# Nine ring slots of weight halves in place of seven, seven of them for the dense part in place of five, and a DMA scratch of 512 bytes

## The chip, the cores and the metric

The kernel runs on one core of one Trainium2 chip. The metric is the device time of one execution in microseconds (us); it was taken in three runs. The core has TensorE (PE, matrix products), VectorE (DVE), ScalarE (ACT), GpSimd (POOL) and SyncE (SP), which here issues nearly all transfers. SBUF is the memory next to the engines, PSUM takes TensorE's results, HBM holds inputs, weights and output. A row of the profile names a line of the kernel file, as L419.

## The reference

Two decoder layers over 256 tokens of width 1024, all in float32. Each has a mixer (differential attention, dilated window attention and gated linear attention side by side), a cross-attention into 256 memory tokens, and a feed-forward part: a dense SwiGLU of width 2816 in layer 0, the best 2 of 8 expert SwiGLUs of width 3584 in layer 1. In short:

```python
for l in range(DEPTH):
    mix = hybrid_mixer(x, positions, w_in[l], ..., w_out[l])
    x = layer_norm(DEEPNORM_ALPHA * x + mix, ln_mix_g[l], ln_mix_b[l])
    xa = memory_cross_attention(x, mem, xa_wq[l], xa_wkv[l], xa_wo[l])
    x = layer_norm(DEEPNORM_ALPHA * x + xa, ln_xa_g[l], ln_xa_b[l])
    if l % 2 == 0:
        f = (silu(x @ w1) * (x @ w3)) @ w2        # ffd_w13, ffd_w2
    else:
        f = moe_swiglu(x, moe_router[0], moe_w13[0], moe_w2[0])
    x = layer_norm(DEEPNORM_ALPHA * x + f, ln_ffn_g[l], ln_ffn_b[l])
```

## The kernel before

The 256 tokens are two tiles of 128 (t = 0 and 1). Weights come in panels of 512 columns, and a panel in two **halves** of 1 MB: 128 partitions x 2048 elements, which is 8 KB per partition. The dense part (all of layer 0, and of layer 1 the mixer and the cross-attention) reads 99 halves, numbered 0 to 98 in `DENSE_HALVES`. Halves 24 to 27 are xa_wq of layer 0, 32 to 55 the up-projections of the dense layer (52 to 55 are only 256 columns wide), 56 to 66 its down-projection, 67 to 78 w_in of layer 1, and 95 to 98 xa_wo of layer 1. The expert part then reads, for each expert, 42 halves numbered q = 0 to 41.

All of them go through one buffer, `ring`, of `RAW_SLOTS` = 7 slots of 8 KB per partition. The dense part uses slots 0 to `DENSE_SLOTS` - 1 = 4. Slot 5 (`DENSE_SLOTS`) is meanwhile the first of four split buffers, `high`, and slot 6 (`RAW_SLOTS` - 1) is scratch room named `spare` (masks of the gated attention, the narrow weights of the forget gate). The expert part uses all 7 slots for its halves. `ring_r` is the same memory as `ring`, seen with the type float32r.

Most products are done in three passes on a split weight: w = w_hi + w_lo, both float32r. ACT casts a half to its high part (L532 in the dense part, into one of the four buffers `high`, whose names in rows are ring_r, late_r, late_r and qk_r; L553 in the expert part, into w_hi). DVE subtracts (L854, in place in the ring; L868, into w_lo). The key, value, w_out and xa_wo weights aren't split; TensorE reads them from the ring as they are. x is cast and subtracted likewise (L520 and L845) after TensorE has transposed it (L1384).

There is no scheduler: each engine runs its own list of instructions in program order, and semaphores order them against each other. What matters here:

- SP issues the halves in their order. `dense` waits, before half `at`, until half `at - DENSE_SLOTS` is used up (`wait_used`, L418). TensorE reports this by `dense_used`, `acc_ready`, `kv_psum` or `w2_ready`, whichever belongs to that half.
- At the end of the dense part SP issues the first six expert halves; those in slots 0 to 4 wait for the last dense half of their slot. Half 6 comes after `load_ln(5)`, which waits for the fifth layer norm (x2 of layer 1); slot 6 is scratch before. From half 7 on each waits for `lo_ready`: DVE has done the half 7 before.
- ACT casts a half once it has landed, and once the half that had its split buffer four split halves before is used up.
- In layer 1, DVE's list has the first expert subtraction, `low(0, 0)`, between the layer norm of tile 0 and the residual sums (L832) and layer norm (L816 to L823) of tile 1 after the cross-attention. ACT's list has three expert casts there, ahead of copying the transposes of x. Then come the router (L1772), the choice of experts, the gather (L1800), and the experts' products (L1819 to L1821).

The order in DVE's list there:

```python
                layer_norm(3 * l + 1, x, 0)
                if l == 0:
                    split_low(1)
                else:
                    low(0, 0)
                residual(l, o_p, 0, 1)
                if l == 0:
                    split_low(1)
                residual(l, o_p, 1, 1)
```

Of the kernel before, what the change touches and what calls it, by code (L numbers as in the profile page):

```python
# [22 lines left out]
F32R = mybir.dt.float32r  # L23
# [4 lines left out]
P = 128  # L28
# [3 lines left out]
KC = D // P  # L32
# [9 lines left out]
CH, CK, CV, CR = 4, 48, 96, 16  # L42
# [9 lines left out]
ROPE = 8  # L52

RAW_SLOTS = 7
DENSE_SLOTS = 5
SPLIT_SLOTS = 3
HALF = KC * N // 2

# [9 lines left out]
DENSE_HALVES = [(l, n, g) for l in range(DEPTH) for n in range(L1 if l == 0 else MIX_PANELS)  # L68
                for g in range(1 if n == L1 - 1 else 2)]
# [50 lines left out]
def bass_decoder(nc, a, out):  # L120
    ctx = ExitStack()
    with ctx:
        def sb(name, shape, dt=F32):
            return ctx.enter_context(nc.sbuf_tensor(name, shape, dt))

        def sem(name):
            return ctx.enter_context(nc.semaphore(name))
# [2 lines left out]


        with ExitStack() as scope:
            ring_r = scope.enter_context(nc.sbuf_tensor("ring_r", [P, RAW_SLOTS, HALF], F32R))
        ring = sb("ring", [P, RAW_SLOTS, HALF])
        ringf = ring[:, :, :].rearrange("p s n -> p (s n)")
        x = sb("x", [P, T, D])
        ln_gb = sb("ln_gb", [P, 2, D])
# [46 lines left out]
        with ExitStack() as scope:  # L184
            def twin(name, shape):
# [30 lines left out]
        o_xa = h[:, :, D:2 * D]  # L216
        cpad = sb("cpad", [P, T, 3 * CH, 64])
        qk = sb("qk", [P, 2, 2, 2 * S])
        spare = ring[:, RAW_SLOTS - 1, :]
        st = spare[:, 0:8 * P].rearrange("p (h b s) -> p h b s", h=2, b=4)  # L220
        stx = spare[:, 8 * P:12 * P].rearrange("p (h b s) -> p h b s", h=2, b=2)

        high = (ring_r[:, DENSE_SLOTS, :], late_r[:, 8192:10240], late_r[:, 12288:14336],
                qk_r[:, :, :, :].rearrange("p m n s -> p (m n s)"))
# [13 lines left out]
        angr = sb("angr", [P, 2, T, ROPE])  # L238
        trig = sb("trig", [P, 2, T, ROPE])
        rt = s4[:, 0, :, 0:T * 24 * 4].rearrange("p n (t k) -> p n t k", t=T)  # L240
        wr_hi, wr_lo = (ring_r[:, RAW_SLOTS - 1, m * KC * CR:(m + 1) * KC * CR].rearrange("p (c r) -> p c r", c=KC)
                        for m in range(2))
        rankT = spare[0:CR, 14 * P:16 * P]
        zz = dec[:, 0:3, 0:T * CH * CK]
# [13 lines left out]
        ln_in = sem("ln_in")  # L258
        dense_in = [sem(f"dense_in{s}") for s in range(DENSE_SLOTS)]
        dense_used = sem("dense_used")  # L260
# [64 lines left out]
        def acc_use(l, n):  # L325
            return l * L1_ACC + (n if n < IN_P else n - KV_P)
# [17 lines left out]
        def dense_src(l, n, g):  # L344

            src = w_panel(l, n)
            c = 2 if n >= L1 - W2_P else 4
            return src[:, c * g:c * (g + 1), :]

        def dense_view(buffer, l, n, g):  # L350
            _, c, w = dense_src(l, n, g).shape
            return buffer[:, 0:c * w].rearrange("p (c n) -> p c n", c=c)

        def raw_half(l, n, g):
            return dense_view(ring[:, HALF_AT[l, n, g] % DENSE_SLOTS, :], l, n, g)

# [3 lines left out]
        def low_half(l, n, g):  # L360
            return dense_view(ring_r[:, HALF_AT[l, n, g] % DENSE_SLOTS, :], l, n, g)

        def half_view(buffer, q, slots):

            return buffer[:, q % slots, :].rearrange("p (c n) -> p c n", c=4 if q < 4 * MOE_PAIRS else 2)
# [13 lines left out]
        def wait_used(engine, index):  # L379


            l, n, g = DENSE_HALVES[index]
            if n == L1 - 1:
                engine.wait_ge(w2_ready, T)
            elif g == 0 or n >= L1 - W2_P:
                own = sum(1 for m, k, c in DENSE_HALVES[:index + 1] if (c == 0 or k >= L1 - W2_P) and k != L1 - 1)
                engine.wait_ge(dense_used, own)
            elif IN_P <= n < IN_P + KV_P:
                engine.wait_ge(kv_psum, 2 * KV_P * l + 2 * (n - IN_P) + 2)
            else:  # L390
                u = acc_use(l, n)
                engine.wait_ge(acc_ready[2 * (u % 2) + 1], u // 2 + 1)
# [8 lines left out]
        @block.sync  # L401
        def _(sp):
            sp.dma_start(x[:, :, :], a["x"][0].rearrange("(t p) d -> p t d", p=P)).then_inc(x_in, 16)
            sp.dma_start(square[:, :, :], a["square"]).then_inc(x_in, 16)

            def load_ln(k):
                l, s = divmod(k, 3)
                g, b = (("ln_mix_g", "ln_mix_b"), ("ln_xa_g", "ln_xa_b"), ("ln_ffn_g", "ln_ffn_b"))[s]
                if k:
                    sp.wait_ge(ln_done, T * k)  # L410
                for n, w in enumerate((g, b)):
                    sp.dma_start(ln_gb[:, n, :], a[w][l:l + 1, :].to_broadcast([P, D])).then_inc(ln_in, 16)

            def dense(l, n):
                for g in range(1 if n == L1 - 1 else 2):
                    at = HALF_AT[l, n, g]
                    if at >= DENSE_SLOTS:
                        wait_used(sp, at - DENSE_SLOTS)  # L418
                    sp.dma_start(raw_half(l, n, g), dense_src(l, n, g)).then_inc(dense_in[at % DENSE_SLOTS], 16)  # L419

            for l in range(DEPTH):
                for n in range(L1 if l == 0 else MIX_PANELS):
                    dense(l, n)
                    if l == 0 and n == 1:
                        sp.dma_start(mem_tok, a["mem"][0].rearrange("(t p) d -> p t d", p=P)).then_inc(mem_in, 16)
                    if n == IN_P + KV_P + OUT_P - 1:
                        load_ln(3 * l)
                    if n == MIX_PANELS - 1:
                        load_ln(3 * l + 1)
                    if n == L1 - 1:  # L430
                        load_ln(3 * l + 2)

            def item_half(q, i, e):

                if q < 4 * MOE_PAIRS:
                    c0 = (q // 2 % 2) * F_MOE + q // 4 * N
                    r = 4 * (q % 2)
                    src = a["moe_w13"][0, e].rearrange("(c p) n -> p c n", p=P)[:, r:r + 4, c0:c0 + N]
                else:
                    r = 2 * (q - 4 * MOE_PAIRS)  # L440
                    src = a["moe_w2"][0, e].rearrange("(c p) n -> p c n", p=P)[:, r:r + 2, :]
                sp.dma_start(half_view(ring, q, RAW_SLOTS), src).then_inc(raw_in[q % RAW_SLOTS], 16)

            def item_halves(i, e, first=0):
                for q in range(first, ITEM_HALVES):
                    sp.wait_ge(lo_ready, ITEM_HALVES * i + (q - RAW_SLOTS + 1))
                    item_half(q, i, e)


            for q in range(RAW_SLOTS - 1):  # L450
                if q < DENSE_SLOTS:
                    last = max(i for i in range(len(DENSE_HALVES)) if i % DENSE_SLOTS == q)
                    wait_used(sp, last)
                item_half(q, 0, 0)
            load_ln(5)
            item_half(RAW_SLOTS - 1, 0, 0)
            item_halves(0, 0, RAW_SLOTS)
            with sp.Fori(1, NE) as i:
                item_halves(i, i)
            sp.wait_ge(table_ready, 1)  # L460
            n_items = sp.value_load(table_i[0:1, 0:1], min_val=NE, max_val=NE + EXTRA)
            with sp.If(n_items > NE):
                with sp.Fori(NE, n_items) as i:
                    e = sp.value_load(table_i[0:1, bass.ds(i - (NE - 1), 1)], min_val=0, max_val=NE - 1)
                    item_halves(i, e)
            sp.wait_ge(ln_done, T * 6)
            sp.dma_start(out[0].rearrange("(t p) d -> p t d", p=P), acc).then_inc(out_done, 16)
            sp.wait_ge(out_done, 16)
# [1445 lines left out]
```

## Time and profile before

| what | value |
|---|---|
| median of three runs | 1912.48 us |
| lowest and highest run | 1912.01 and 1916.35 us |
| span of the profiled execution (first to last instruction) | 1910.2 us |
| busy: PE, DVE, ACT, POOL | 94%, 68%, 51%, 1% |
| mean granted TensorE clock | 0.968 |
| HBM over the span | 244 GB/s |
| transfers of dense halves, issue to landing | about 5.0 us each |

The page gives the span of the profiled execution; its time as a run is not listed apart, and no run is below 1912.01 us. Busy shares are means over stages with different limits: in the first 860 us or so, the dense part, transfers take some 10 to 60% of the DMA engines' time in all slices but the first, and after it 90% and more in most. What a slot of the ring is worth must be read at the single places where an engine waits for a transfer. A row of the chain of waits gives a start, a duration and what ran; where the next row starts at once, the step was released by the one before it. In a timeline the bracket at the end of a row is the idle time of the engine before it, and what ended it.

### The profile page before, as it was taken

The numbers are of one execution on the slowest core, as the hardware profiler recorded it, in microseconds if no ns is written. First come the engines' busy times: TensorE is split into PE (matmuls) and PEld (weight loads), VectorE is DVE, ScalarE is ACT, GpSimd is POOL, SyncE is SP. The second block draws the span as 40 slices with busy tenths as digits, with TensorE's granted clock in tenths as the row PEclk, the third lists the DMA queues.
The fourth block names the chain that finished last, engine by engine and source line by source line (L and its number), as shares of the span: only waits on it lengthen the run. The fifth ranks groups of instructions, "written<-read, shape, count | busy, mean of one in ns | idle before, by whom it ended". The sixth has DMA issues, their size and how long they took to land.

```text
span 1910.2 us, 21467 instructions
## 1 busy us (share of the span) xinstructions
PE 1791.2 (94%) x7962; PEld 1385.8 (73%) x7962; DVE 1298.7 (68%) x1209; ACT 975.6 (51%) x853; POOL 13.8 (1%) x22
## 2 busy tenths in 40 slices
PE   7998889999899989979999999999999999999996
PEld 6846575788776475647887878878878778788785
DVE  4465434445463555258988888889889788898896
ACT  4333122444333312216766667667667676676673
POOL 0000000000000000000000000000000000000000
PEclk9998899999999969979999999999999999999998
DMA  8523232545534312267999989999999999999991
GB/s 283 177 88 111 67 132 88 180 173 186 211 132 153 112 67 88 89 242 255 363 348 322 370 321 344 338 327 371 339 324 371 332 331 335 326 370 341 322 370 63
DMA packets 206471, 466.19 MB, mean 244 GB/s; under 512 B 11952, under 2 KB 14416, under 8 KB 206416
## 3 DMA queue, kind: packets, MB, share of 16 engines
q1 hardware_dynamic: 200880, 463.76, 67.7%
q10 hardware_dynamic: 5536, 1.68, 0.4%
q8 instruction: 36, 0.59, 0.1%
q14 instruction: 19, 0.16, 0.0%
HBM read 464.36 MB, written 1.05 MB: 244 GB/s over the span
## 4 chain that ended last, share of the span: by engine, by line
PE 85%; DVE 6%; ACT 4%; issue 4%; DMA 1%; POOL 0%; DVEq 0%; SPq 0%; ACTq 0%
PE ps L1423 21%; PE ps L1819 15%; PE ps L1821 15%; PE ps L1820 15%; PE ps L1450 6%; PE ps L1741 3%; ACT w_hi L553 3%; PE ps L1809 1%; PE ps L1800 1%; PE ps L1614 1%; DVE w_lo L868 1%; PE ps L1831 1%; PE ps L1667 1%; PE ps L1649 1%; PE ps L1384 1%
## 5 line engine op out<-in xcount | busy, mean ns | idle before, releaser
L868 DVE TENSOR_TENSOR w_lo<-ring,w_hi 128x2048 fp32r<-128x2048 f32 x336 | 768.6, 2289 | 163.9 <-ACT w_hi L553 163.4
L553 ACT CAST w_hi<-ring 128x2048 fp32r<-128x2048 f32 x336 | 641.7, 1910 | 329.9 <-PE ps L1821 316.8
L1819 PE MATMUL ps<-w_hi,xe_hi 128*128 128x512 f32 x896 | 364.5, 407 | 2.7 <-DVE xe_lo L1271 1.4
L1821 PE MATMUL ps<-w_hi,xe_lo 128*128 128x512 f32 x896 | 349.7, 390 | 0.0
L1820 PE MATMUL ps<-w_lo,xe_hi 128*128 128x512 f32 x896 | 348.9, 389 | 0.0
L1819 PEld LDWEIGHTS ps<-w_hi,xe_hi 128*128 128x128 f32 x896 | 168.3, 188 | 43.4 <-issue 8.3
L1820 PEld LDWEIGHTS ps<-w_lo,xe_hi 128*128 128x128 f32 x896 | 168.4, 188 | 40.0 <-issue 6.7
L1821 PEld LDWEIGHTS ps<-w_hi,xe_lo 128*128 128x128 f32 x896 | 168.1, 188 | 36.1
L1819 PE MATMUL ps<-w_hi,he_hi 128*128 128x512 f32 x448 | 177.5, 396 | 0.0
L1821 PE MATMUL ps<-w_hi,he_lo 128*128 128x512 f32 x448 | 174.8, 390 | 0.0
L1820 PE MATMUL ps<-w_lo,he_hi 128*128 128x512 f32 x448 | 174.4, 389 | 0.0
L1423 PE MATMUL ps<-ring_r,xT_r 128*128 128x512 f32 (+1 forms) x560 | 149.4, 398 | 11.7 <-DVE late_r L845 6.8
L1423 PEld LDWEIGHTS ps<-ring_r,xT_r 128*128 128x128 f32 x560 | 105.3, 193 | 35.9 <-DVE late_r L845 7.6
L1423 PE MATMUL ps<-ring,xT 128*128 128x512 f32 x256 | 116.1, 611 | 9.3 <-ACT xT L510 6.3
L1450 PE MATMUL ps<-ring,memT 128*128 128x512 f32 x256 | 116.4, 598 | 0.1
L1423 PEld LDWEIGHTS ps<-ring,xT 128*128 128x128 f32 x256 | 49.8, 197 | 69.3 <-issue 62.5
L1821 PEld LDWEIGHTS ps<-w_hi,he_lo 128*128 128x128 f32 x448 | 84.1, 188 | 18.0
L1820 PEld LDWEIGHTS ps<-w_lo,he_hi 128*128 128x128 f32 x448 | 84.3, 188 | 16.6
L1819 PEld LDWEIGHTS ps<-w_hi,he_hi 128*128 128x128 f32 x448 | 84.2, 188 | 16.4
L532 ACT CAST late_r<-ring 128x2048 fp32r<-128x2048 f32 (+1 forms) x34 | 63.0, 1858 | 63.1 <-DMA ring<-in_xa_wq_dram 20.4
L854 DVE TENSOR_TENSOR ring_r<-ring,late_r 128x2048 fp32r<-128x2048 f32 (+1 forms) x34 | 75.5, 2227 | 27.1 <-ACT late_r L532 26.2
L1450 PEld LDWEIGHTS ps<-ring,memT 128*128 128x128 f32 x256 | 46.2, 190 | 50.9 <-issue 49.5
(258 smaller groups left out, 1834.3 us busy)
## 6 DMA issues: line engine op xcount, KB each, us to landing
ring<-in_moe_w_dram SPq DMA_DIRECT2D x336, 1024.0 KB, 5.0
ring<-in_ffd_w_dram SPq DMA_DIRECT2D x31, 1024.0 KB, 5.0
ring<-in_w_in_dram SPq DMA_DIRECT2D x24, 1024.0 KB, 5.1
ring<-in_xa_wkv_dram SPq DMA_DIRECT2D x16, 1024.0 KB, 4.9
ring<-in_w_out_dram SPq DMA_DIRECT2D x8, 1024.0 KB, 5.0
ring<-in_xa_wq_dram SPq DMA_DIRECT2D x8, 1024.0 KB, 5.0
ring<-in_xa_wo_dram SPq DMA_DIRECT2D x8, 1024.0 KB, 5.1
ring<-in_ffd_w_dram SPq DMA_DIRECT2D x4, 512.0 KB, 3.6
```

The costliest lines, as they stand in the source:

```text
L532: act.copy(high_half(*name), raw_half(*name)).then_inc(dense_hi, 1)
L553: act.copy(w_hi[:, q % SPLIT_SLOTS, :], ring[:, q % RAW_SLOTS, :]).then_inc(hi_ready, 1)
L854: dve.tensor_tensor(low_half(*name), raw_half(*name), high_half(*name).bitcast(F32), ALU.subtract).then_inc(dense_lo, 1)
L868: dve.tensor_tensor(w_lo[:, q % SPLIT_SLOTS, :], ring[:, q % RAW_SLOTS, :], w_hi[:, q % SPLIT_SLOTS, :].bitcast(F32), ALU.subtract).then_i ...
L1384: ins = pe.transpose(ps[:, 4 + b, c * P:(c + 1) * P], src[:, t, k * P:(k + 1) * P], ident)
L1423: ins = pe.matmul(ps[:, b, 0:w], lhs[:, 4 * g + c, t * P:(t + 1) * P], rhs[:, c, :], start=(g == 0 and m == 0 and c == 0), stop=(g == 1 an ...
L1450: ins = pe.matmul(ps[:, piece_bank(i), :], memT[:, k, t * P:(t + 1) * P], raw_half(l, IN_P + n, g)[:, c, :], start=(k == 0), stop=(k == KC ...
L1614: ins = pe.matmul(ps[:, 4 + 2 * hp + s % 2, at:at + P], k[:, t * P:(t + 1) * P], q[:, tq * P:(tq + 1) * P], start=True, stop=True)
L1741: ins = pe.matmul(ps[:, t + 2 * col, :], (h_hi, h_lo)[p][:, k, t * P:(t + 1) * P], weights[q][:, c, col * N:(col + 1) * N], start=(k == 0 ...
L1819: pe.matmul(ps[:, bank, :], x_hi, hi[:, c, cols], start=first, stop=False)
L1820: pe.matmul(ps[:, bank, :], x_hi, lo[:, c, cols], start=False, stop=False)
L1821: return pe.matmul(ps[:, bank, :], x_lo, hi[:, c, cols], start=False, stop=last)
```

## The change

- `DENSE_SLOTS` is 7, and a new `RING_SLOTS` = `DENSE_SLOTS` + 2 = 9 is the size of `ring` and `ring_r`: 16 KB per partition more. The dense part goes round over slots 0 to 6. The split buffer `high[0]` is slot 7, and `spare` slot 8.
- `RAW_SLOTS` stays 7: the expert part uses slots 0 to 6.
- The first seven expert halves now each wait for the last dense half of their slot, and all seven come before `load_ln(5)`.
- The DMA scratch (`dynamic_dma_scratch_size`) is set to 512 bytes, where the argument was left at its default.

```diff
--- before.py
+++ after.py
@@ -52,7 +52,8 @@
 ROPE = 8
 
 RAW_SLOTS = 7
-DENSE_SLOTS = 5
+DENSE_SLOTS = 7
+RING_SLOTS = DENSE_SLOTS + 2
 SPLIT_SLOTS = 3
 HALF = KC * N // 2
 
@@ -130,8 +131,8 @@
 
 
         with ExitStack() as scope:
-            ring_r = scope.enter_context(nc.sbuf_tensor("ring_r", [P, RAW_SLOTS, HALF], F32R))
-        ring = sb("ring", [P, RAW_SLOTS, HALF])
+            ring_r = scope.enter_context(nc.sbuf_tensor("ring_r", [P, RING_SLOTS, HALF], F32R))
+        ring = sb("ring", [P, RING_SLOTS, HALF])
         ringf = ring[:, :, :].rearrange("p s n -> p (s n)")
         x = sb("x", [P, T, D])
         ln_gb = sb("ln_gb", [P, 2, D])
@@ -216,7 +217,7 @@
         o_xa = h[:, :, D:2 * D]
         cpad = sb("cpad", [P, T, 3 * CH, 64])
         qk = sb("qk", [P, 2, 2, 2 * S])
-        spare = ring[:, RAW_SLOTS - 1, :]
+        spare = ring[:, RING_SLOTS - 1, :]
         st = spare[:, 0:8 * P].rearrange("p (h b s) -> p h b s", h=2, b=4)
         stx = spare[:, 8 * P:12 * P].rearrange("p (h b s) -> p h b s", h=2, b=2)
 
@@ -238,7 +239,7 @@
         angr = sb("angr", [P, 2, T, ROPE])
         trig = sb("trig", [P, 2, T, ROPE])
         rt = s4[:, 0, :, 0:T * 24 * 4].rearrange("p n (t k) -> p n t k", t=T)
-        wr_hi, wr_lo = (ring_r[:, RAW_SLOTS - 1, m * KC * CR:(m + 1) * KC * CR].rearrange("p (c r) -> p c r", c=KC)
+        wr_hi, wr_lo = (ring_r[:, RING_SLOTS - 1, m * KC * CR:(m + 1) * KC * CR].rearrange("p (c r) -> p c r", c=KC)
                         for m in range(2))
         rankT = spare[0:CR, 14 * P:16 * P]
         zz = dec[:, 0:3, 0:T * CH * CK]
@@ -447,13 +448,11 @@
                     item_half(q, i, e)
 
 
-            for q in range(RAW_SLOTS - 1):
-                if q < DENSE_SLOTS:
-                    last = max(i for i in range(len(DENSE_HALVES)) if i % DENSE_SLOTS == q)
-                    wait_used(sp, last)
+            for q in range(RAW_SLOTS):
+                last = max(i for i in range(len(DENSE_HALVES)) if i % DENSE_SLOTS == q)
+                wait_used(sp, last)
                 item_half(q, 0, 0)
             load_ln(5)
-            item_half(RAW_SLOTS - 1, 0, 0)
             item_halves(0, 0, RAW_SLOTS)
             with sp.Fori(1, NE) as i:
                 item_halves(i, i)
@@ -1899,7 +1898,7 @@
     import concourse.bacc as bacc
     from concourse.bass_utils import run_bass_kernel_spmd as run
 
-    nc = bacc.Bacc("TRN2", target_bir_lowering=False, num_devices=1)
+    nc = bacc.Bacc("TRN2", target_bir_lowering=False, num_devices=1, dynamic_dma_scratch_size=512)
     given = {name: np.ascontiguousarray(inputs[name]) for name in _INS}
     given.update(shape_constants())
     arrays, args = {}, {}
```

ACT, DVE, TensorE and GpSimd keep their instructions and their order; what changes for them is which slot and which of now seven `dense_in` semaphores a half has. SP's list changes at every wait of the dense part, in the same way: it waits for the half 7 before, not 5 before. Two places of it follow.

SP's queue from the last narrow up-projection halves to the first w_in halves of layer 1, before:

```order
L419 DMA ring<-in_ffd_w13_dram 128x4x256 [waits acc_ready1]
L419 DMA ring<-in_ffd_w13_dram 128x4x256 [waits dense_used]
L419 DMA ring<-in_ffd_w2_dram 128x2x1024 [waits acc_ready3]
L419 DMA ring<-in_ffd_w2_dram 128x2x1024 [waits dense_used]
L419 DMA ring<-in_ffd_w2_dram 128x2x1024 [waits acc_ready1]
L419 DMA ring<-in_ffd_w2_dram 128x2x1024 [waits dense_used]
L419 DMA ring<-in_ffd_w2_dram 128x2x1024 [waits acc_ready3]
L419 DMA ring<-in_ffd_w2_dram 128x2x1024 [waits dense_used] x6
L412 DMA ln_gb<-in_ln_ffn_g_dram 128x1024 [waits ln_done]
L412 DMA ln_gb<-in_ln_ffn_b_dram 128x1024
L419 DMA ring<-in_w_in_dram 128x4x512 [waits dense_used] x4
L419 DMA ring<-in_w_in_dram 128x4x512 [waits w2_ready]
```

The same place of the changed kernel (line numbers are one higher):

```order
L420 DMA ring<-in_ffd_w2_dram 128x2x1024 [waits acc_ready1]
L420 DMA ring<-in_ffd_w2_dram 128x2x1024 [waits dense_used]
L420 DMA ring<-in_ffd_w2_dram 128x2x1024 [waits acc_ready3]
L420 DMA ring<-in_ffd_w2_dram 128x2x1024 [waits dense_used]
L420 DMA ring<-in_ffd_w2_dram 128x2x1024 [waits acc_ready1]
L420 DMA ring<-in_ffd_w2_dram 128x2x1024 [waits dense_used]
L420 DMA ring<-in_ffd_w2_dram 128x2x1024 [waits acc_ready3]
L420 DMA ring<-in_ffd_w2_dram 128x2x1024 [waits dense_used] x4
L413 DMA ln_gb<-in_ln_ffn_g_dram 128x1024 [waits ln_done]
L413 DMA ln_gb<-in_ln_ffn_b_dram 128x1024
L420 DMA ring<-in_w_in_dram 128x4x512 [waits dense_used] x6
L420 DMA ring<-in_w_in_dram 128x4x512 [waits w2_ready]
```

Each half now carries the wait that the half two places ahead of it carried before: of the w_in halves six instead of four wait for `dense_used`, that is for halves inside the down-projection, ahead of the one that waits for its end (`w2_ready`).

SP's queue at the end of the cross-attention of layer 1, where the expert halves begin (in_moe_w13), before:

```order
L412 DMA ln_gb<-in_ln_xa_g_dram 128x1024 [waits ln_done]
L412 DMA ln_gb<-in_ln_xa_b_dram 128x1024
L442 DMA ring<-in_moe_w13_dram 128x4x512 [waits dense_used]
L442 DMA ring<-in_moe_w13_dram 128x4x512 [waits acc_ready1]
L442 DMA ring<-in_moe_w13_dram 128x4x512 [waits dense_used]
L442 DMA ring<-in_moe_w13_dram 128x4x512 [waits acc_ready3] x2
L442 DMA ring<-in_moe_w13_dram 128x4x512
L412 DMA ln_gb<-in_ln_ffn_g_dram 128x1024 [waits ln_done]
L412 DMA ln_gb<-in_ln_ffn_b_dram 128x1024
L442 DMA ring<-in_moe_w13_dram 128x4x512
L442 DMA ring<-in_moe_w13_dram 128x4x512 [waits lo_ready] x21
```

The same place of the changed kernel:

```order
L413 DMA ln_gb<-in_ln_xa_g_dram 128x1024 [waits ln_done]
L413 DMA ln_gb<-in_ln_xa_b_dram 128x1024
L443 DMA ring<-in_moe_w13_dram 128x4x512 [waits acc_ready3]
L443 DMA ring<-in_moe_w13_dram 128x4x512 [waits acc_ready1]
L443 DMA ring<-in_moe_w13_dram 128x4x512 [waits dense_used]
L443 DMA ring<-in_moe_w13_dram 128x4x512 [waits acc_ready3]
L443 DMA ring<-in_moe_w13_dram 128x4x512 [waits dense_used]
L443 DMA ring<-in_moe_w13_dram 128x4x512 [waits acc_ready1]
L443 DMA ring<-in_moe_w13_dram 128x4x512 [waits dense_used]
L413 DMA ln_gb<-in_ln_ffn_g_dram 128x1024 [waits ln_done]
L413 DMA ln_gb<-in_ln_ffn_b_dram 128x1024
L443 DMA ring<-in_moe_w13_dram 128x4x512 [waits lo_ready] x21
```

The first expert half waited for `dense_used` of half 95, the first half of the last but one panel. Now it waits for `acc_ready3`, which TensorE gives at its last product of the dense part (half 98). The other six waits are for halves 92 to 97, and the seventh half stands ahead of the layer norm weights.

## Rows read from the trace of the kernel before

**Rows 1.** The page, part 4: the chain by engine

```profile
PE 85%; DVE 6%; ACT 4%; issue 4%; DMA 1%; POOL 0%; DVEq 0%; SPq 0%; ACTq 0%
```

**Rows 2.** The chain, 430 to 545: start us, us, what

```profile
445.44 4.92 DMA ring<-in_ffd_w_dram
...
456.04 4.31 PE ps L1741 x12
...
516.48 5.41 DMA ring<-in_w_in_dram
...
521.91 1.90 ACT late_r L532
...
524.41 0.70 DVE late_r L845
...
525.80 13.54 PE ps L1423 x48
```

**Rows 3.** The chain, 821 to 841

```profile
821.43 4.89 DMA ring<-in_moe_w_dram
...
826.40 1.91 ACT w_hi L553
...
828.34 2.29 DVE w_lo L868
...
837.73 1.96 PE ps L1384 x8
```

**Rows 4.** Waits, 0 to 850 and 860 to 1910: us, times, longest us

```profile
PE ps L1423 <- DVE late_r L845: 17.5, 8, 5.7
...
ACT w_hi L553 <- PE ps L1821: 316.8, 331, 5.2
```

**Rows 5.** SP's timeline (start, us, what); landings of its first, then of the next two

```profile
831.73 1.47 SPq L442 DMA_DIRECT2D ring<-in_moe_w_dram  x3
...
DMA to landing us min/median/max: 5.1/5.1/5.1
...
DMA to landing us min/median/max: 7.3/8.4/9.5
```

**Rows 6.** Windows: us, PE PEld DVE ACT POOL busy (x), PEclk, DMA share, GB/s

```profile
525.00:530.00 5.00, 4.20 (x10) 3.37 (x11) 5.00 (x4) 0.00 (x0) 0.00 (x0) 0.50 0.01 3
...
840.00:845.00 5.00, 4.45 (x21) 4.48 (x22) 4.80 (x3) 0.00 (x0) 0.00 (x0) 0.50 1.03 388
```

**Rows 7.** Timeline of DVE from 450: start us, us, what, idle before

```profile
452.32 2.29 DVE L854 TENSOR_TENSOR ring_r<-ring,late_r 128x2048 fp32r<-128x2048 f32 x1 [0.68 <-ACT late_r L532]
```

**Rows 8.** Timeline of SP's queue, from 446.5 and from 496

```profile
446.86 0.37 SPq L419 DMA_DIRECT2D ring<-in_ffd_w_dram  x1
...
496.97 0.38 SPq L419 DMA_DIRECT2D ring<-in_w_in_dram  x1
```

**Rows 9.** Timeline of DVE from 519

```profile
519.26 0.69 DVE L1216 SCALAR_TENSOR_TENSOR x<-x,ps 128x512 f32<-128x512 f32 x1 [2.29 <-PE ps L1741]
...
521.43 0.69 DVE L1217 BATCH_NORM_STATS2 stats<-x 128x6 f32<-128x512 f32 x1
```

**Rows 10.** Timelines of ACT from 231 and of DVE from 237

```profile
231.88 1.90 ACT L532 CAST late_r<-ring 128x2048 fp32r<-128x2048 f32 x1 [20.38 <-DMA ring<-in_xa_wq_dram]
...
237.18 0.69 DVE L832 SCALAR_TENSOR_TENSOR x<-x,ps 128x512 f32<-128x512 f32 x1 [1.00 <-PE ps L1423]
```

**Rows 11.** The chain at 43, and ACT's timeline from 27

```profile
43.18 44.57 PE ps L1423 x192
...
27.14 5.04 ACTq L570 DMA_DIRECT2D ring<-in_w_in_dram  x2
...
35.09 1.91 ACT L532 CAST ring_r<-ring 128x2048 fp32r<-128x2048 f32 x1 [0.17 <-ACT h L498]
```

**Rows 12.** The page, part 3: the two queues that carry the kernel's data

```profile
q1 hardware_dynamic: 200880, 463.76, 67.7%
...
q10 hardware_dynamic: 5536, 1.68, 0.4%
```

## The prediction

> **What bounds the kernel now.** I read the chain that ended last first, then the waits, then the transfers' issue and landing times at the places where a transfer stands on that chain. The chain is 85% TensorE and only 1% DMA [rows 1]. A deeper ring of weight slots can give back only what stands there as DMA, or what ACT and DVE do late because of it. The reader is to see three such places: 445.44 (a half of the dense layer's down-projection), 516.48 (first weights of the second layer) and 821.43 (first expert weights) [rows 2, 3]. Behind the last one comes the expert part, more than half of the span; there ACT waits 316.8 us in 331 pieces for TensorE to free a split buffer [rows 4], so ring and transfers are ahead of TensorE and the part shifts as a whole with its start. It keeps 7 slots in both kernels.
>
> **The hand-over to the experts, the largest term.** What changes is which dense half had the slot before. The 99 dense halves are numbered 0 to 98, and a half goes to the slot of its number modulo the dense slots. With 5, expert half 0 takes slot 0 after half 95, half 1 follows 96, half 2 follows 97, half 3 follows 98. With 7, slot 0 held half 98, the very last one; expert halves 1 to 6 follow 92 to 97, but stand behind half 0 in SP's queue. So all seven wait until TensorE has finished the last dense product.
> When is that? Half 95 is used up at 821.43, where expert half 0 is issued [rows 3]; half 98 at 831.73, where SP issues half 3, which waits for it today, and two more [rows 5]. The first expert transfer moves by 831.73 - 821.43 = 10.30 us.
> What hangs on it: the transfer (4.89), ACT's cast to w_hi (1.91 from 826.40), DVE's subtraction to w_lo (2.29 from 828.34), and behind that in DVE's queue both residual sums of token tile 1 and its layer norm, then TensorE's transposes at 837.73 [rows 3]. Each step follows the one before at once, and TensorE's last product, which the second sum needs, is over by then. No slack absorbs the delay: +10.30. Router, top-2 choice, gather and all experts come after.
> Does the landing change with seven transfers queued? Three are issued today within 1.47 us from 831.73: the first lands after 5.1 us, at 836.8, the third after 9.5 us, by 842.2, so they are some 2.7 us apart [rows 5]. The first does not wait for those behind it. Half 0 then lands at 836.8, half 2 at 842.2, and ACT is through its three casts at 844.1, before the transposes of x, at 837.73 + 10.30 = 848.0, need it. I take 0; the upper bound is 9.5 - 5.1 = 4.4 us, as if the first landed like the third.
> The Trainium skill (DMA: Bandwidth & Descriptors, Bandwidth) gives 6.15 us for a 1 MB transfer from HBM. By that figure half 0 would land 1.05 us later than by the row, and the hand-over would cost an estimated 11.4 us in place of 10.3; the row has 5.1 us, and it decides.
> SP goes on to the norm weights and half 7 once the layer norm is done, 10.3 us later too; TensorE's expert start moves as far, so the lead of the ring stays.
>
> **The longer TensorE pause there.** The idle stretch before 837.73 grows by 10.3 us. In 840 to 845, behind today's pause, the granted clock is already 0.50, that is 1.2 GHz [rows 6]; the router and the gather run behind a fallen clock in both kernels. I take 0, with 1.7 us either way for a fall or rise that comes earlier or later.
> The Trainium skill (TensorE: Matmul & The Clock Gate, What's actually happening) has the throttled clock as the default, released by activity, which speaks against a change that makes TensorE idle longer. By that rule the loss would exceed the shift only if work behind today's pause ran at the full clock; the row shows that it does not.
>
> **What the dense part wins.** Each half is issued once the half 7 before it, not 5 before it, is used up: two halves earlier.
> At 445.44 half 57 is issued, and lands 4.92 later [rows 2]. With 7 slots it goes two halves sooner; its split buffer is free when half 53 is used up, at 446.86 [rows 8], so ACT can cast right behind its previous cast. Today DVE idles 0.68 us for that cast before its subtraction at 452.32 [rows 7]; then come the gating products that free the last PSUM bank, and TensorE starts at 456.04 [rows 2]. With the transfer gone DVE is the bound: -0.68.
> At 516.48 half 70 is issued, once half 65 is used; it lands after 5.41, ACT casts for 1.90 from 521.91 and then casts x; DVE subtracts x at 524.41, and TensorE starts at 525.80 [rows 2]. With 7 slots half 69 goes at 496.97, where 67 goes today [rows 8], and half 70 when half 63 is used. From half 65 used (516.48) to half 66 used (519.26 [rows 9]) is 2.78 us, so half 63 is used at 510.9 and half 70 lands by 516.4. Next late is the split buffer: there are four, so the cast of half 70 waits for half 66, at 519.26, when DVE also gets its residual sums [rows 9]. ACT ends that cast at 521.2 and the first x cast some 0.6 later; DVE is busy with sums and statistics until 521.43 + 0.69 = 522.12 [rows 9]. So DVE's x subtraction starts at 522.15 in place of 524.41: -2.26.
> TensorE's granted clock is 0.50 in 525 to 530 [rows 6]. The 48 products from 525.80 take 13.54 us, and 192 of that kind take 44.57 at the start, so 48 would take 11.1 [rows 2, 11]. Started 2.3 us sooner, TensorE may meet more or less of the slow stretch: 2.4 us at most are to be won, and I set 1.7 as the loss. I take 0.
>
> **Where it wins nothing.** ACT waits 20.38 us for a half of xa_wq before 231.88. But DVE's residual sum at 237.18 waits for TensorE, not for ACT, whose cast is long done [rows 10]. The second layer has the same code.
> At the start two more ring transfers go out at once. They use the engines for 2 x 2.7 = 5.4 us while ACT issues its constants (the last two end at 27.14 + 5.04). If that held ACT up by all of it, its cast of 35.09 would end at 42.4, DVE's subtraction at 44.7, and the products of 43.18 would start 1.5 us late [rows 11]. Value 0, upper bound 1.5, nothing below.
> The scratch: all kernel data goes by q1 and q10, both hardware_dynamic (463.76 and 1.68 MB) [rows 12], issued by SP and ACT; GpSimd issues none. I take 0 for 512 bytes; a loss would show as slower landings everywhere.
>
> **Sum.** +10.30 - 0.68 - 2.26 = +7.36 us. The profiled span is 1910.2, the median of the runs 1912.48; the 2.3 us between them are taken to lie around the span and stay. 1912.48 + 7.36 = 1919.8 us.
>
> **Rivals.** A, the forecast: 1917.4 (2.4 us of clock won) to 1923.2 (1.7 us lost at both places). Chance 0.63, of which 0.10 comes out within 0.3% (5.7 us, about what a measurement here can tell from no change).
> B, the dense part wins nothing, because something that I count as ready, a split buffer or DVE's queue, is late in place of the transfer: +10.30, 1922.8. For it: four split buffers against seven slots. Against: DVE's rows at 519 to 522 [rows 9]. Chance 0.14.
> C, a dear start (+1.5) or shared landing (+4.4) on top of the sum: 1921.3 to 1924.2. Against the second: the landings at 831.73 [rows 5]. Chance 0.08.
> D, not slower: TensorE waits 17.5 us in 8 places for DVE's x subtraction at the layer norms [rows 4]. If there the transfers hold ACT and DVE up, the deeper ring shortens all eight. From 7.4 us on, less than half of it, that pays for the hand-over; at 10 us the sum is -2.6, 1909.8. For it: ACT's wait of 20.38 us right before one of the places. Against: DVE waits for TensorE at 237.18 [rows 10]. Chance 0.15, 0.06 of it faster, 0.09 within.
> Faster 0.06, same 0.10 + 0.09 = 0.19, slower 0.75. Range 1915.0 to 1924.5: down into D and the clock, up over B and C.
>
> **What would show it.** Right: SP's first expert transfer starts where TensorE's last dense product ends, near 828.8 (831.73 - 2.94); its half lands 4.9 to 5.2 us after; ACT, DVE and TensorE follow in today's order. TensorE starts the down-projection near 455.4 and the second layer near 522.9. ACT's 20 us wait for xa_wq is gone and the layer norm behind it comes no sooner. The expert part takes as long as before. Wrong: the second layer's start stays put (B), the gaps at the layer norms shrink (D), or half 0 lands over 6 us after its issue (C).

## The result, and the profile after

| kernel | median us | runs | ratio to the kernel before, 95% interval |
|---|---|---|---|
| before, beside it | 1912.24 | 4 | |
| changed | 1922.47 | 4 | 1.0045 (1.0032 to 1.0057) |
| before, beside the repeat | 1913.93 | 21 | |
| changed, repeated | 1920.37 | 5 | 1.0037 (1.0024 to 1.0051) |

The change makes the kernel slower, by 8.6 us (6.1 to 10.9) in the first comparison and by 7.1 us (4.6 to 9.8) in the repeat, working the ratios out on the two medians of before. The forecast was 1919.8 us, 7.4 us slower. The ratios are those on record and aren't the quotients of the medians: the medians in this table differ by 10.2 and 6.4 us.

The hand-over to the experts, in the chain of the changed kernel (start us, us, what); it answers to [rows 3]:

```profile
818.76 13.98 PE ps L1422 x32
...
832.76 5.06 DMA ring<-in_moe_w_dram
...
837.90 1.91 ACT w_hi L552
...
839.84 2.29 DVE w_lo L867
...
849.23 1.95 PE ps L1383 x8
...
852.05 6.98 PE ps L1771 x32
```

The reader is to see that the chain now goes through all 32 instructions of the last dense products and only then to the transfer: it starts at 832.76, where TensorE ends. Before, it left TensorE after 8 of them, at 821.43. From the start of these products to the router it takes 852.05 - 818.76 = 33.29 us, and took 22.82 (817.73 to 840.55 in the chain of before): +10.47.

Seven transfers go out together now. SP's timeline of the changed kernel from 832, and the landings of the first two and of the second and third, which answer to [rows 5]:

```profile
832.76 6.86 SPq L443 DMA_DIRECT2D ring<-in_moe_w_dram  x6
...
DMA to landing us min/median/max: 5.1/6.2/7.4
...
DMA to landing us min/median/max: 7.4/8.4/9.5
```

The first still lands after 5.1 us, the second after 7.4, the third after 9.5. It does not wait for those behind it.

The dense layer and the start of the second layer, in the chain of the changed kernel; it answers to [rows 2]:

```profile
443.70 5.66 PE ps L1422 x48
...
449.94 1.92 ACT ring_r L531
...
454.09 2.28 DVE ring_r L853
...
457.80 4.58 PE ps L1740 x12
...
521.29 0.70 DVE x L1215
...
523.46 0.70 DVE stats L1216
...
524.19 0.70 DVE late_r L844
...
525.58 12.98 PE ps L1422 x48
```

No row with DMA stands in this stretch any more. At both places DVE works without a gap up to TensorE's start: the second subtraction (454.09) right behind the first, and x's subtraction (524.19) right behind the statistics.

The waits of the changed kernel, 0 to 850 and from 865 (us, times, longest us), answering to [rows 4]:

```profile
PE ps L1422 <- DVE late_r L844: 15.2, 8, 3.5
ACT w_hi L552 <- DMA ring<-in_moe_w_dram: 22.0, 3, 20.5
...
ACT w_hi L552 <- PE ps L1820: 316.9, 331, 5.1
```

TensorE's waits at the layer norms fell from 17.5 to 15.2 us, and the longest of them from 5.7 to 3.5: the 2.3 us are the second layer's start alone. ACT's one long wait for a transfer is now the hand-over. Its wait for TensorE in the expert part is what it was.

Two rows of ACT in the changed kernel, at xa_wq of layer 0 (it answers to [rows 10]) and at the start of the second layer:

```profile
240.09 1.07 ACT L519 CAST xT_r<-ps 128x512 fp32r<-128x512 f32 x2 [24.75 <-PE ps L1383]
...
523.15 1.07 ACT L519 CAST xT_r<-ps 128x512 fp32r<-128x512 f32 x2
```

In the first, ACT waits for TensorE's transposes of x, no longer for a transfer. In the second, two casts of x take 1.07 us together, so I estimate that the first is done near 523.7, while DVE takes x up at 524.19: ACT, and with it the split buffer that it had to wait for, is ahead of DVE there by about 0.5 us.

### The profile page after: what moved, and what is told of

It is laid out like the page before. It is cut to its first block, busy times and chain, and to the rows that moved or that the text cites. A ratio compares the mean times of both kernels' runs of the same rounds, so it can differ in the third digit from the quotient of the medians.

```text
span 1920.9 us, 21467 instructions
## 1 busy us (share of the span) xinstructions
PE 1796.0 (93%) x7962; PEld 1388.1 (72%) x7962; DVE 1297.9 (68%) x1209; ACT 974.7 (51%) x853; POOL 13.8 (1%) x22
## 4 chain that ended last, share of the span: by engine, by line
PE 85%; DVE 7%; ACT 4%; issue 3%; DMA 1%; POOL 0%; DVEq 0%; SPq 0%; ACTq 0%
PE ps L1422 22%; PE ps L1818 15%; PE ps L1820 14%; PE ps L1819 14%; PE ps L1449 6%; PE ps L1740 3%; ACT w_hi L552 3%; PE ps L1808 1%; PE ps L1613 1%; DVE w_lo L867 1%; PE ps L1799 1%; PE ps L1830 1%; PE ps L1666 1%; PE ps L1648 1%; PE ps L1383 1%
## 5 line engine op out<-in xcount | busy, mean ns | idle before, releaser
L552 ACT CAST w_hi<-ring 128x2048 fp32r<-128x2048 f32 x336 | 641.7, 1910 | 339.0 <-PE ps L1820 316.9
L1449 PE MATMUL ps<-ring,memT 128*128 128x512 f32 x256 | 120.3, 615 | 0.1
L853 DVE TENSOR_TENSOR ring_r<-ring,late_r 128x2048 fp32r<-128x2048 f32 (+1 forms) x34 | 75.3, 2225 | 18.5 <-ACT late_r L531 17.5
```

The source lines that it names most:

```text
L552: act.copy(w_hi[:, q % SPLIT_SLOTS, :], ring[:, q % RAW_SLOTS, :]).then_inc(hi_ready, 1)
L853: dve.tensor_tensor(low_half(*name), raw_half(*name), high_half(*name).bitcast(F32), ALU.subtract).then_inc(dense_lo, 1)
L1449: ins = pe.matmul(ps[:, piece_bank(i), :], memT[:, k, t * P:(t + 1) * P], raw_half(l, IN_P + n, g)[:, c, :], start=(k == 0), stop=(k == KC ...
```

## Where the time went, in stretches of all profiles

Every profile's chain has the same landmarks: (a) the 192 products that begin near 43 us, (b) the first products of the dense layer, (c) of its down-projection, (d) of the second layer, (e) the run of 240 products in it, (f) the last 32 product instructions of the dense part, (g) the router. Differences of their starts, in us; the names of the experiments are those of the next section:

| profile | slots | a to b | b to c | c to d | d to e | e to f | f to g |
|---|---|---|---|---|---|---|---|
| before | 5 | 280.0 | 132.83 | 69.76 | 16.27 | 275.66 | 22.82 |
| e9 (before again) | 5 | 282.5 | 132.83 | 70.02 | 16.22 | 275.65 | 22.97 |
| e2 (scratch) | 5 | 282.6 | 132.92 | 70.24 | 16.21 | 275.65 | 23.01 |
| e3 (late wait) | 5 | 282.6 | 132.99 | 69.94 | 16.34 | 275.74 | 33.31 |
| changed | 7 | 282.8 | 132.09 | 67.78 | 15.70 | 277.48 | 33.29 |
| e5 (changed again) | 7 | 279.6 | 133.63 | 67.79 | 15.70 | 276.92 | 33.42 |
| e1 (turned by 1) | 7 | 281.1 | 132.08 | 67.77 | 15.68 | 276.81 | 22.58 |
| e7 (turned by 6) | 7 | 281.1 | 132.04 | 67.79 | 15.70 | 276.81 | 29.84 |
| e4 (six slots) | 6 | 282.2 | 132.05 | 67.80 | 15.70 | 275.64 | 26.49 |
| e6 (six, turned) | 6 | 282.5 | 132.03 | 67.78 | 15.70 | 274.02 | 22.53 |
| e8 (five split buffers) | 6 | 280.3 | 132.22 | 66.34 | 16.54 | 277.56 | 22.54 |

The columns b to c, c to d, d to e and f to g follow the kernel to half a microsecond, save where a slow clock stretch falls otherwise (b to c in e5, c to d and d to e in e8, told below). The column a to b does not follow it: it differs by 3.2 us between the two profiles of the changed kernel, and by 2.5 between those of the kernel before. The column e to f differs by 0.6 and 0.0 us between the same pairs, and by 3.5 between e6 and e8, which have the same dense slots; both are taken up in the section on the prediction.

## The experiments

**e1: the change, with expert half q in ring slot (q + 1) mod 7.** Half 98's slot then goes to expert half 6.

```diff
-            return buffer[:, q % slots, :].rearrange(...)
+            at = (q + TURN_BY) % slots if slots == RAW_SLOTS else q % slots
+            return buffer[:, at, :].rearrange(...)
-                last = max(i for i in ... if i % DENSE_SLOTS == q)
+                last = max(i for i in ... if i % DENSE_SLOTS == (q + TURN_BY) % RAW_SLOTS)
```

(and the same index where ACT and DVE read the ring; `TURN_BY` = 1)

> The change with one difference: expert half q takes ring slot (q + 1) mod 7 in place of q mod 7, so that the slot of the last dense half (98) goes to expert half 6, and halves 0 to 5 follow dense halves 92 to 97. Theory (the hand-over costs the change 10.3 us because expert half 0 waits for half 98): the first expert transfer is issued well before TensorE's last dense product, ACT does not wait for it, and DVE's second residual sum follows that product at once, some 0.3 us sooner after it than in the kernel before. The rest is the dense part's win, 2.0 to 3.3 us. Time 3 us below the kernel before (1908 to 1910.5) and 11 to 13 us below the change. Rival (the loss comes from the deeper ring itself, by slower or shared transfers, or from clock stretches that the changed dense part brings about): no more than half of the 10 us is regained, the time stays above 1915.

Measured: 1910.16 us against 1914.49, ratio 0.9975 (0.9966 to 0.9984). That is 4.8 us faster than before, and 12 to 13 us below the change by the ratios. Its chain at the hand-over:

```profile
816.50 13.99 PE ps L1424 x32
...
830.60 0.70 DVE x L833
...
836.26 1.95 PE ps L1385 x8
...
839.08 6.98 PE ps L1773 x32
```

and ACT's timeline there, where the bracket at the end is the idle time before:

```profile
815.07 5.51 ACT L554 CAST w_hi<-ring 128x2048 fp32r<-128x2048 f32 x3
830.95 0.58 ACT L511 COPY xT<-ps 128x512 f32<-128x512 f32 x1 [10.37 <-PE ps L1385]
```

No transfer stands on the chain. ACT casts all three halves at once at 815, 1.4 us before the last dense products begin, and DVE's second residual sum follows TensorE's end by 0.1 us. The stretch f to g is 22.58 us, 10.7 below the change's and 0.2 to 0.4 below that of the three undelayed profiles with five slots. With the 3.6 us of b to e that makes 4.0 us by the stretches; the runs have 4.8 (3.1 to 6.5). This shows that the loss was the slot order, not the deeper ring.

**e2: the kernel before, with the scratch of 512 bytes alone.**

```diff
-    nc = bacc.Bacc("TRN2", target_bir_lowering=False, num_devices=1)
+    nc = bacc.Bacc("TRN2", target_bir_lowering=False, num_devices=1, dynamic_dma_scratch_size=512)
```

> The kernel before with the DMA scratch of 512 bytes alone, ring untouched. Theory: no difference, within 0.2% of the kernel before, transfers landing after 4.9 to 5.1 us as there. Rival (the scratch is part of the loss): 2 to 10 us slower, landings above 5.3 us.

Measured: 1917.19 us against 1914.49, ratio 1.0009 (1.0000 to 1.0019), that is 1.8 us (0 to 3.6): the interval touches no difference. The runs lie in two groups, four from 1912.06 to 1914.74 us and six from 1917.16 to 1917.99, and the profile is of a run of the first (1914.35). Its transfers, from part 6 of its page (the last number is the median from issue to landing), took 0.0 to 0.3 us longer than before:

```profile
ring<-in_moe_w_dram SPq DMA_DIRECT2D x336, 1024.0 KB, 5.2
ring<-in_ffd_w_dram SPq DMA_DIRECT2D x31, 1024.0 KB, 5.2
ring<-in_w_in_dram SPq DMA_DIRECT2D x24, 1024.0 KB, 5.4
```

That is above the 4.9 to 5.1 us expected, but e9, which has the old scratch, shows 5.1, 5.1 and 5.3 in these rows, and e3, also with the old scratch, 5.2, 5.2 and 5.3: the excess does not belong to the scratch. In its stretches b to g it stands within 0.25 us of e9, the kernel before again, each. A loss of 2 us or more that belongs to the scratch is not seen in any stretch of this profile. By the runs alone up to 3.6 us are not excluded; against as much stand e1, e6 and e8, which have the small scratch and are 4 to 5 us faster than the kernel before, no less than the 4 us that their shorter stretches give.

**e3: the kernel before, where expert half 0 waits for dense half 98 in place of 95.**

```diff
-                    wait_used(sp, last)
+                    wait_used(sp, last if q else len(DENSE_HALVES) - 1)
```

> The kernel before, five dense slots, seven in all, with one wait changed: expert half 0 waits for dense half 98 in place of 95. Theory: this wait alone is the cost of the hand-over, 10.3 to 10.7 us, with none of the dense part's win: 1922 to 1923.5. Rival (part of the step is due to seven transfers at once, or the dense part already lags): under 8 us.

Measured: 1923.27 us against 1914.49, ratio 1.0052 (1.0038 to 1.0066), so 10.0 us (7.3 to 12.6). The stretch f to g is 33.31 us, the same as the change's 33.29:

```profile
820.51 13.99 PE ps L1423 x32
...
834.52 5.07 DMA ring<-in_moe_w_dram
```

One wait, in a kernel with five slots and the old scratch, costs the whole hand-over. The columns from b to e stay at the five-slot values.

**e4: the change with six dense slots, eight in all.**

```diff
-DENSE_SLOTS = 7
+DENSE_SLOTS = 6
-                last = max(i for i in ... if i % DENSE_SLOTS == q)
-                wait_used(sp, last)
+                if q < DENSE_SLOTS:
+                    last = max(i for i in ... if i % DENSE_SLOTS == q)
+                    wait_used(sp, last)
```

(expert half 6, whose slot held a split buffer, has no wait of its own; it stands in SP's queue behind the waits of the others)

> The change with six dense slots, eight in all. Dense halves are then issued one later than in the change, one earlier than before; expert half 0 waits for half 96, half 1 for 97, half 2 for 98. Theory: hand-over 3.44 us late (half 96 used at 824.87 against 821.43), the same win in the dense part, since half 70 then lands at 519.1, just as its split buffer comes free: sum 0 to +1.5 us against the kernel before. Rival (depth itself costs, in proportion): half of the change's loss, +5 us.

Measured: 1914.09 us against 1914.49, ratio 1.0001 (0.9992 to 1.0010). Its chain at the hand-over:

```profile
815.41 7.12 PE ps L1423 x16
822.55 5.12 DMA ring<-in_moe_w_dram
...
841.90 6.98 PE ps L1772 x32
```

The chain leaves TensorE after 16 of the 32 instructions, once half 96 is used up: f to g is 26.49, 3.5 us above the 22.93 that is the mean of before, e9 and e2. The dense part's win is there in full, and the two cancel.

**e5: the changed kernel once more.** No edit.

> The changed kernel itself once more, beside more runs of the kernel before on the same chip. The first comparison gave +0.45% (0.32 to 0.57), more than the forecast sum of 7.4 us. Theory (the sum is right and the rest was chance, TensorE's slow clock stretches falling otherwise in single executions): +0.3 to +0.45%, 6 to 9 us, and in its profile the stretch from 43 us to the start of the dense layer does not always carry the 2.5 us that it carried in the first profile. Rival (the deeper ring itself slows the mixers, by about 2.5 us): +0.5% or more, and the first 325 us as long as in the first profile.

Measured: 1920.37 us, ratio 1.0037 (1.0024 to 1.0051); the stretch a to b took 279.6 us, 3.2 less than in the first profile of the same kernel. The windows of 105 to 125 us of the changed kernel's two profiles and of e9, one line each in that order (PE, PEld, DVE, ACT, POOL busy, then the granted clock):

```profile
105.00:125.00 20.00, 18.29 (x69) 9.28 (x68) 11.02 (x33) 5.86 (x20) 0.00 (x0) 0.91 0.32 106
```

```profile
105.00:125.00 20.00, 18.29 (x72) 9.37 (x71) 12.41 (x35) 5.92 (x21) 0.00 (x0) 1.00 0.29 106
```

```profile
105.00:125.00 20.00, 18.28 (x69) 9.33 (x68) 11.02 (x33) 5.71 (x20) 0.00 (x0) 0.91 0.32 106
```

In the first profile of the change and in e9, but not in e5 nor in the first profile of before (where the same window shows 1.00), the clock fell for a moment here, and TensorE got through 69 instructions in place of 72. The rival, a ring that slows the mixers, falls for this stretch. Between b and c it is the other way round: the 48 products at b take 12.95 us in e5, with the clock at 0.86 in 320 to 325, and 11.40 us in the first profile, with 1.00; that is the 1.5 us by which b to c is longer in e5.

**e6: six dense slots, and half q in slot (q + 3) mod 7.** The edit is shown against e1.

```diff
-DENSE_SLOTS = 7
-TURN_BY = 1
+DENSE_SLOTS = 6
+TURN_BY = 3
```

(slot 6, the first split buffer, waits for the last split half that lay in it)

> Six dense slots, eight in all, and expert half q in slot (q + 3) mod 7, so that half 98's slot goes to expert half 6. Theory: hand-over as in the turned version with seven dense slots, and the dense part's win is the same with six slots as with seven, since the four split buffers bound it: the same time as the turned version, 3 to 5 us below the kernel before (ratio 0.997 to 0.9985). Rival (each slot more gives its own share): half the win, ratio 0.9985 or above.

Measured: 1909.14 us against 1913.93, ratio 0.9979 (0.9970 to 0.9988). The dense columns are those of seven slots. With the turned order six slots do what seven do, with 8 KB per partition less.

**e7: seven dense slots, turned by six.** Expert half 0 follows half 97. The edit is shown against e1.

```diff
-TURN_BY = 1
+TURN_BY = 6
```

> Seven dense slots, expert half q in slot (q + 6) mod 7: expert half 0 follows dense half 97, which is used up 3.43 us before half 98, and half 1 follows half 98. Theory (the cost is the distance of the half that expert half 0 waits for, nothing else): hand-over 6.9 us later than in the kernel before in place of 10.3, less 3.3 us of win in the dense part: +3 to +4.5 us against the kernel before, 3.4 us below the change. Rival (what counts is that all seven are queued behind TensorE's end, or several land late together): as slow as the change, +8 us.

Measured: 1917.38 us against 1913.93, ratio 1.0020 (1.0011 to 1.0029), 3.8 us. Its chain:

```profile
816.35 10.55 PE ps L1424 x24
826.91 5.05 DMA ring<-in_moe_w_dram
...
846.19 6.98 PE ps L1773 x32
```

24 of the 32 instructions, then the transfer; f to g is 29.84. Against the mean of 22.93, waiting for half 96, 97 or 98 costs 3.56 (e4), 6.91 (e7) and 10.36 to 10.49 us (changed, e5), where the experiments' expectations had 3.44 and 6.9 and the prediction 10.30. All seven are queued one behind the other in e7 too; only the half waited for differs.

**e8: e6 with a fifth split buffer.**

```diff
-RING_SLOTS = DENSE_SLOTS + 2
-HIGH_SLOTS = 4
+RING_SLOTS = DENSE_SLOTS + 3
+HIGH_SLOTS = 5
-        high = (ring_r[:, DENSE_SLOTS, :], late_r[:, 8192:10240], ...
+        high = (ring_r[:, DENSE_SLOTS, :], ring_r[:, DENSE_SLOTS + 1, :], late_r[:, 8192:10240], ...
-                    by_tile = last + 1 - HIGH_SLOTS
+                    by_tile = last + 1 - 4
```

(the last edit keeps TensorE's order of the down-projection as it was)

> The six-slot turned version with a fifth split buffer (nine slots in all), so that the cast of the last half for the second layer waits for half 65 in place of 66 and is 2.8 us sooner. Theory (DVE's residual sums and statistics after the down-projection end as late as ACT's cast chain, and bound TensorE's start): no gain, TensorE starts the second layer 67.8 us after the down-projection as with four buffers, time as the six-slot turned version (ratio 0.997 to 0.999 to the kernel before). Rival (the split buffer is what is late next): another 1 to 2.5 us there.

Measured: 1910.00 us against 1914.30, ratio 0.9976 (0.9966 to 0.9986), as e6. In the profile c to d is 66.34, 1.4 less than the expected 67.8, but the buffer does not give it. Its chain at the start of the down-projection:

```profile
455.79 3.04 PE ps L1744 x12
...
459.26 58.55 PE ps L1744 x252
```

The first 12 products take 3.04 us, where the changed kernel's row of 457.80 has 4.58: no slow clock there this time (1.00 over 455 to 462, against 0.76). Behind d it is the other way round: 48 products take 13.82 us against 12.98, which makes d to e longer. From the 252 products on it is 522.13 - 459.26 = 62.87 us, against 525.58 - 462.81 = 62.77 in the changed kernel. DVE's timeline of e8 at that place:

```profile
520.01 0.69 DVE L1220 BATCH_NORM_STATS2 stats<-x 128x6 f32<-128x512 f32 x1
520.74 1.29 DVE L848 TENSOR_TENSOR late_r<-ps,xT_r 128x512 fp32r<-128x512 f32 x2
```

x's subtraction follows the statistics without a gap: DVE is the bound. With six slots ACT's casts there wait for their transfers again (3.33 and 1.54 us before the last two), so the run does not show what a fifth buffer does beside seven.

**e9: the kernel before once more, one profile.** No edit.

> The kernel before once more, one profile, to see how TensorE's slow clock stretches fall in another execution of the same program. Theory (they fall by chance): the stretch from 43 us to the dense layer's first product differs from the first profile's 280.0 us by 1 to 2.5 us, with slow stretches at other places, while the pieces between differ by less than 0.2 us. Rival (they are fixed by the program): the same places as in the first profile.

Measured: 1914.02 us, span 1912.2. The stretch a to b is 282.5 us against 280.0, and its slow clock at 105 to 125 us stands above. The four columns between b and f agree within 0.26 us between the two profiles, a little more than the 0.2 expected, and within 0.5 us over the four profiles with five slots.

## Why the prediction was right, step by step

- **Hand-over, +10.30.** Right. The profiles have +10.47 from the first profile of before, and 10.36 to 10.49 from the mean of three. e3 shows it by one wait alone, e1 by taking it away, e4 and e7 by its steps. The small excess is the landing: the changed kernel's transfer takes 5.06 us where before had 4.89 [rows 3]. The 11.4 us that the prediction works out beside it from the Trainium skill (DMA: Bandwidth & Descriptors, Bandwidth) is not a rival sum: the table of that section is for transfers issued from GpSimd, where SP issues these, and a slower landing would stand in the chain of both kernels and leave the shift as it is.
- **Landings with seven queued, 0.** Right: 5.1, 7.4 and 9.5 us, as of three [rows 5]. The 4.4 us of the upper bound did not come.
- **The longer pause of TensorE, taken as 0.** No loss came. The 0.8 us by which the next item is shorter are in the gather: its 32 products take 5.88 us in the first profile of the change against 6.72 before. The pause does not set this: e3, with the same late hand-over, has 6.60, as e9 without it has 6.59. It lies within the bound of 1.7.
- **Expert part, unchanged.** Right: from the router to DVE's last normalizing instruction 1063.0 us against 1063.8 before, and ACT's wait for TensorE 316.9 against 316.8 us. From the router to the end of the span it is 1068.8 to 1069.7 us in all eleven profiles.
- **Down-projection, -0.68.** 132.06 us (mean of changed, e1, e4, e6, e7) against 132.89 (before, e9, e2, e3) from b to c: -0.83. DVE's idle time of 0.68 [rows 7] is gone, as the chain after shows.
- **Second layer's start, -2.26.** 67.78 against 69.99: -2.21. The step that names what is late next was right too: DVE's sums and statistics, which end about 0.5 us after ACT's first cast of x, and so after all that the split buffer holds up (ACT's row of 523.15 above).
- **The clock behind it, taken as 0.** Mis-sized. From d to e it is 15.70 against 16.26 us, -0.56: started sooner, the 48 products take 12.98 in place of 13.54. It lies within the bounds of -2.4 and +1.7.
- **Nothing at xa_wq, at the start, or elsewhere.** ACT's 20 us wait is gone; instead it waits 24.75 us for TensorE's transposes of x before its next cast, at 240.09. The layer norm behind it comes no sooner: a to b takes 279.6 to 282.8 us with seven slots and 280.0 to 282.6 with five, and what differs there is TensorE's own time, as shown below. Nor does the start lose: a lies at 42.66 to 43.05 us with seven slots, at 42.39 to 43.18 with five. The stretch e to f needs a closer look: 277.5, 276.9, 276.8 and 276.8 us in four profiles with seven slots, 275.6 to 275.7 in five with five or six, but 274.0 and 277.6 in two others with six. Adding up the chain's pieces by engine settles where this is. In all eleven profiles DVE's pieces take 24.18 to 24.21 us there, ACT's 6.02 to 6.04 and the pieces named issue 7.29 to 7.33; only TensorE's differ, from 234.5 us (e6) to 238.0 (changed, e8), with 236.1 before. So nothing waits longer or less; the same products take longer or less. Two pairs of rows show it, each before and then changed, the second pair with e5:

```profile
661.83 5.35 PE ps L1450 x12
```

```profile
662.09 7.58 PE ps L1449 x12
```

```profile
751.63 12.94 PE ps L1423 x48
```

```profile
751.68 11.40 PE ps L1422 x48
```

The granted clock is 1.00 and 0.74 over 655 to 665 in the first pair, 0.89 and 1.00 over 750 to 765 in the second. The stretch a to b is of the same kind: DVE 26.28 to 26.32 us, ACT 6.01 to 6.05 and issue 7.82 to 7.86 in all eleven, TensorE 237.4 (e5) to 240.7 (changed). What stays open is whether the deeper ring has a part in where the clock falls: e5, e1 and e7 are alike from e to f, but the first profile of the change is like e8, with six slots.

- **Sum.** By the stretches +10.4 - 0.83 - 2.21 - 0.56 = +6.8 us, the forecast had +7.36, the two comparisons 8.6 and 7.1. The spans of the first two profiles differ by 10.7: in the order of the table -0.3 ahead of a, then +2.8, -0.7, -2.0, -0.6, +1.8 and +10.5, and -0.8 behind g. The +2.8 and +1.8 are where the clock happened to fall: the first profile of before had the shortest a to b of the five-slot kernels. The four runs of before in the first comparison had a median of 1912.24, and the larger sets beside the experiments 1913.93 (21 runs) to 1914.49 (27 runs).

The forecast of 1919.8 us started from a median of three runs, 1912.48, which is 1.5 to 2.0 us below the medians of the larger sets. That it lies 0.6 us from the repeat (1920.37) and 2.7 from the first comparison (1922.47) is in part luck; what it can be held to is the difference of 7.4 us.

The rivals: B (nothing won, +10.3) is refuted by the columns b to e. C needs landings that did not come, or a later a, which did not come either. D needed the eight waits at the layer norms; only one of them shrank, because DVE waits there for TensorE, as [rows 10] had it.

The runs point to a version that beats both kernels: the deeper ring with the expert halves' slots turned, e1 (0.9975), e6 (0.9979) or e8 (0.9976), which these runs do not tell apart. By memory e6 is the cheapest.

## What to carry to other kernels

When a ring changes its number of slots, look at both its ends: the slot of the next stage's first buffer may belong to the last thing that the stage before uses, and everything queued behind that wait goes with it. A turn of the slot numbers costs no memory and no instruction and was worth 10.7 us here, more than the 3.6 us of the deeper ring. How deep a ring needs to be is read from what is late next: with four split buffers and DVE's list behind it, the sixth dense slot gave all and the seventh nothing.

## What the runs showed of the hardware that I had not expected

The granted clock falls at other places in executions of the same program. The two profiles of the changed kernel differ by 3.2 us between 43 us and the dense layer, those of the kernel before by 2.5, with the clock at 0.91 in one and 1.00 in the other over 105 to 125 us. The times of 27 runs of the kernel before lie between 1910.37 and 1918.12 us. A change of 5 us can be read from the stretches of one profile that the change touches, once rows with a fallen clock in them are set apart (1.5 us in b to c of e5), and not from one profile's span.
